# Left and right token half by turns for each weight tile, in place of one half after the other

## The reference

```python
def layer(x, ...):
    h = rmsnorm(x, norm_mix_g)
    p = h @ w_in                                # 2048 x 5120
    u = gelu(p[u]); v = rmsnorm(gelu(p[v]), sgu_norm_g)
    y_a = u * chunk_sgu(v, w_s, b_s)
    zc, new_mix = causal_dwconv(cg * xb, mix_prev, conv_mix_w, conv_mix_b)
    y = concat(group_rmsnorm(y_a), group_rmsnorm(bg * zc))
    x = x + y @ w_out                           # 2048 x 2048
    h = rmsnorm(x, norm_ffn_g)
    gate, new_ffn = causal_dwconv(h @ w_gate, ffn_prev, conv_ffn_w, conv_ffn_b)   # 2048 x 5632
    x = x + (silu(gate) * (h @ w_up)) @ w_down  # 2048 x 5632, 5632 x 2048
    return x, new_mix, new_ffn, v
```

## Time and profile before

| | us |
|---|---|
| median of 3 runs | 2511.51 |
| lowest, highest | 2509.65, 2513.96 |
| span of the profiled execution | 2507.9 |
| TensorE busy | 2462.1 (98%) |
| VectorE busy | 1206.8 (48%) |
| ScalarE busy | 617.1 (25%) |
| GpSimd busy | 160.2 (6%) |
| mean DMA rate | 87 GB/s |

### The profile page before, as it was taken

How to read it: one execution, slowest core, us unless ns; L and a number is a source line. 1 busy time by engine, 2 the same in 40 slices (tenths; PEclk the granted TensorE clock), 3 DMA queues, 4 the chain that set the end, 5 groups by cost and what they waited for, 6 DMA issues and landing times.

```text
span 2507.9 us, 45612 instructions
## 1 busy us (share of the span) xinstructions
PE 2462.1 (98%) x18473; PEld 2452.1 (98%) x18473; DVE 1206.8 (48%) x1902; ACT 617.1 (25%) x738; POOL 160.2 (6%) x279
## 2 busy tenths in 40 slices
PE   6999999999999999999999999999999999999996
PEld 6999999999999999999999999999999999999996
DVE  6357644556224535455434444444544354454445
ACT  6224312113113322222212222122222211222224
POOL 3310000001221000000000000000000000000004
PEclk8999999999999999999999999999999999999998
DMA  5422222224222222223222222222232222222222
GB/s 153 159 84 71 69 85 85 83 85 151 83 79 73 84 80 81 84 84 92 75 84 84 84 84 81 80 80 82 78 97 78 76 84 84 84 84 84 84 85 84
DMA packets 326837, 219.17 MB, mean 87 GB/s; under 512 B 6804, under 2 KB 301839, under 8 KB 324992
## 3 DMA queue, kind: packets, MB, share of 16 engines
q1 hardware_dynamic: 324432, 203.98, 27.2%
q0 software_dynamic: 2352, 14.41, 1.6%
HBM read 208.19 MB, written 10.18 MB: 87 GB/s over the span
## 4 chain that ended last, share of the span: by engine, by line
PE 96%; ACT 1%; DVE 1%; POOL 0%; issue 0%; DMA 0%; POOLq 0%; SPq 0%; DVEq 0%; ACTq 0%
PE ps L1161 32%; PE ps L1163 31%; PE ps L1162 31%; DVE h_lo L797 0%; POOL acc L470 0%; ACT ps L540 0%; PE ps L1284 0%; ACT h_hi L512 0%; PE ps L1297 0%; DMA x_nat<-in_x_prompt_dram 0%; ACT X L520 0%; PE ps L1296 0%; ACT w_hi L491 0%; DVE rms L813 0%; PE ps L1276 0%
## 5 line engine op out<-in xcount | busy, mean ns | idle before, releaser
L1161 PE MATMUL ps<-h_hi,w_hi 128*128 128x288 f32 x4608 | 1362.2, 296 | 6.2 <-issue 4.9
L1163 PE MATMUL ps<-h_hi,w_lo 128*128 128x288 f32 x4608 | 1358.7, 295 | 0.0
L1162 PE MATMUL ps<-h_lo,w_hi 128*128 128x288 f32 x4608 | 1358.3, 295 | 0.0
L1161 PEld LDWEIGHTS ps<-h_hi,w_hi 128*128 128x128 f32 x4608 | 865.6, 188 | 8.4 <-issue 5.8
L1162 PEld LDWEIGHTS ps<-h_lo,w_hi 128*128 128x128 f32 x4608 | 865.7, 188 | 0.0
L1163 PEld LDWEIGHTS ps<-h_hi,w_lo 128*128 128x128 f32 x4608 | 865.7, 188 | 0.0
L771 DVE TENSOR_TENSOR w_lo<-raw,w_hi 128x1024 fp32r<-128x1024 f32 x376 | 460.5, 1248 | 305.7 <-ACT w_hi L491 305.6
L491 ACT ACTIVATE w_hi<-raw 128x1024 fp32r<-128x1024 f32 x376 | 384.2, 1050 | 489.9 <-PE ps L1163 474.5
L1161 PE MATMUL ps<-act_hi,w_hi 128*128 128x288 f32 x1408 | 418.4, 297 | 1.0 <-DVE scaled L781 1.0
L1163 PE MATMUL ps<-act_hi,w_lo 128*128 128x288 f32 x1408 | 415.0, 295 | 0.0
L1162 PE MATMUL ps<-act_lo,w_hi 128*128 128x288 f32 x1408 | 414.3, 294 | 0.0
(11 more groups left out here) (184 smaller groups left out, 921.6 us busy)
## 6 DMA issues: line engine op xcount, KB each, us to landing
raw<-in_w_gate_dram SPq DMA_DIRECT2D x88, 512.0 KB, 3.9
raw<-in_w_up_dram SPq DMA_DIRECT2D x88, 512.0 KB, 3.8
raw<-in_w_down_dram SPq DMA_DIRECT2D x88, 512.0 KB, 4.3
raw<-in_w_in_dram SPq DMA_DIRECT2D x80, 512.0 KB, 4.3
raw<-in_w_out_dram SPq DMA_DIRECT2D x32, 512.0 KB, 4.0
xT_scratch<-X POOLq DMA_DIRECT2D x1, 4608.0 KB, 18.5
X<-xT_scratch POOLq DMA_DIRECT2D x4, 1152.0 KB, 5.6
x_nat<-in_x_prompt_dram SPq DMA_DIRECT2D x4, 1024.0 KB, 8.6
```

Of the source, the lines that this page charges most:

```text
L1161: te.matmul(out, whi, xhi, start=start, stop=False)
L1162: te.matmul(out, whi, xlo, start=False, stop=False)
L1163: return te.matmul(out, wlo, xhi, start=False, stop=stop)
```

## The change

The helper `three` becomes `three_pairs`: it takes both halves of the input and makes the three products of the left half, then the three of the right half, for one weight tile. `gemm` and `down_tile` call it block by block, so the bank changes with every third matmul. In `gemm` the wait for the second piece moves from the 25th matmul to the 49th, and the signal for the first piece from the 72nd to the 48th. The hooks stay at the same counts. `gemm2_by_k` calls the new helper too, and its order is the same as before. The first gemm of the kernel, which starts before all of x is there, gets a function of its own with the old order. The order of the sums for each output value is as before.

```diff
-            def three(out, whi, wlo, xhi, xlo, start, stop):
-
-                te.matmul(out, whi, xhi, start=start, stop=False)
-                te.matmul(out, whi, xlo, start=False, stop=False)
-                return te.matmul(out, wlo, xhi, start=False, stop=stop)
-
-            def gemm(q, c, p, q1=None, mid=None, q3=None):
-
+            def three_pairs(p, whi, wlo, xhi, xlo, start, stop):
 
                 for half in range(2):
                     cols = slice(half * HALF, (half + 1) * HALF)
-                    for s in range(2):
-                        if half == 0:
-                            pe.wait_ge(lo_ready, q + s + 1)
-                        for k in range(PK):
-                            kk = s * PK + k
-                            last = three(pair(p, half), w_hi[:, (c + s) % 4, k, :], w_lo[:, (c + s) % 4, k, :],
-                                         h_hi[:, kk, cols], h_lo[:, kk, cols], kk == 0, kk == KT - 1)
-                        if half == 1:
+                    te.matmul(pair(p, half), whi, xhi[:, cols], start=start, stop=False)
+                    te.matmul(pair(p, half), whi, xlo[:, cols], start=False, stop=False)
+                    last = te.matmul(pair(p, half), wlo, xhi[:, cols], start=False, stop=stop)
+                return last
+
+            def gemm(q, c, p, q1=None, mid=None, q3=None):
+
+
+                for s in range(2):
+                    pe.wait_ge(lo_ready, q + s + 1)
+                    for k in range(PK):
+                        kk = s * PK + k
+                        last = three_pairs(p, w_hi[:, (c + s) % 4, k, :], w_lo[:, (c + s) % 4, k, :],
+                                           h_hi[:, kk, :], h_lo[:, kk, :], kk == 0, kk == KT - 1)
+                        hook = (q1, q3)[s] if k == PK // 2 - 1 else mid if s == 0 and k == PK - 1 else None
+                        if k == PK - 1:
                             last.then_inc(piece_done, 1)
-                        hook = (q1, mid, q3, None)[2 * half + s]
                         if hook is not None:
                             hook()
+
+            def first_gemm(q, c, p, mid):
+
+                for half in range(2):
+                    cols = slice(half * HALF, (half + 1) * HALF)
+                    for kk in range(KT):
...
@@
-                        for half in range(2):
-                            cols = slice(half * HALF, (half + 1) * HALF)
-                            last = three(pair(tile, half), w_hi[:, c, k, :], w_lo[:, c, k, :],
-                                         h_hi[:, kk, cols], h_lo[:, kk, cols], kk == 0, kk == KT - 1)
+                        last = three_pairs(tile, w_hi[:, c, k, :], w_lo[:, c, k, :],
+                                           h_hi[:, kk, :], h_lo[:, kk, :], kk == 0, kk == KT - 1)
@@
-            gemm(0, 0, 0, mid=rest_of_x)
+            first_gemm(0, 0, 0, rest_of_x)
@@
-                for half in range(2):
-                    cols = slice(half * HALF, (half + 1) * HALF)
-                    for k in ks:
-                        last = three(pair(p, half), w_hi[:, slot, 4 * k + jj, :], w_lo[:, slot, 4 * k + jj, :],
-                                     act_hi[:, k, cols], act_lo[:, k, cols], k == 0, k == 1)
+                for k in ks:
+                    last = three_pairs(p, w_hi[:, slot, 4 * k + jj, :], w_lo[:, slot, 4 * k + jj, :],
+                                       act_hi[:, k, :], act_lo[:, k, :], k == 0, k == 1)
```

More of the change, by code:

```diff
@@ L1178, in gemm @@
                             last.then_inc(piece_done, 1)
-                        hook = (q1, mid, q3, None)[2 * half + s]
                         if hook is not None:
                             hook()
+            def first_gemm(q, c, p, mid):
+                for half in range(2):
+                    cols = slice(half * HALF, (half + 1) * HALF)
+                    for kk in range(KT):
+                        s, k = kk // PK, kk % PK
+                        if half == 0 and k == 0:
+                            pe.wait_ge(lo_ready, q + s + 1)
+                        w, lo = w_hi[:, c + s, k, :], w_lo[:, c + s, k, :]
+                        te.matmul(pair(p, half), w, h_hi[:, kk, cols], start=kk == 0, stop=False)
+                        te.matmul(pair(p, half), w, h_lo[:, kk, cols], start=False, stop=False)
+                        last = te.matmul(pair(p, half), lo, h_hi[:, kk, cols], start=False, stop=kk == KT - 1)
+                        if half == 1 and k == PK - 1:
+                            last.then_inc(piece_done, 1)
+                    if half == 0:
+                        mid()
```

## The result

The changed kernel takes 2523.67 us (median of 4 runs, 2523.22 to 2524.16), beside 2511.1 us for the kernel before (4 runs, 2509.65 to 2513.96): 12.6 us more. The ratio is 1.0047, with a 95% interval of 1.0033 to 1.0061. The forecast was 2524.6 us.

A forecast was written before the change was run, and what follows sets the result against it. The prediction took TensorE's start-to-start matmul distance to bound the kernel. Its terms, 11.1 + 2.4 - 0.4 = +13.1 us on a 2507.9 us span, gave 2521.0, or 2524.6 us as median, range 2517 to 2527 us (0.79).

The forecast's parts named there:

- What bounds the kernel: Whole kernel: TensorE busy 98% of 2507.9 us, so the start-to-start distance over 18048 matmuls decides the time.
- gemm, +11.1 us: In gemm, 13344 matmuls go from 132.50 to 133.33 ns, the distance read in gemm2_by_k: +11.1 us.
- The price of down_tile: Rival for gemm and down_tile: each pair of bank changes costs 3.1 ns, +7.6 us in all, 2519.1 us; chance 0.19.
- down_tile, +2.4 us: In down_tile, 348 tiles of twelve matmuls go from 1593.1 to 1600.0 ns each: +2.4 us.
- The second piece's wait, -0.4 us: In the second gate tile, TensorE's wait at the 25th matmul for the second weight piece goes away: -0.4 us.
- Earlier release, both banks opened at once, hooks: 0: In gemm, first piece released 3.2 us earlier, right bank opened with the left, hooks at unchanged counts: each costs 0.
- The sum: Whole kernel: 11.1 + 2.4 - 0.4 = +13.1 us on the 2507.9 us span, so 2521.0; median 2524.6 us.
- More changes of bank, longer distance.: Across gemm, down_tile and gemm2_by_k, more frequent bank changes lengthen the distance: 132.50, 132.76 and 133.33 ns.
- The free change: Rival: bank change costs nothing, gemms stay at 132.50 ns, decided by under 132.9 ns; 2511.1 us; chance 0.13.
- the dearer visit: Rival: returning to a bank after three matmuls costs twice gemm2_by_k's price, +26.6 us, 2538 us; chance 0.05.
- The gain of both halves at 131.7: Rival in gemm: right half falls to the left half's distance, 6672 matmuls gain 1.4 ns, -9.3 us, 2501.8 us; chance 0.03.

The follow-up runs named there:

- the cut at 272: Kernel before in its own order, tokens cut at column 272 (left 272, right 304 columns) instead of evenly: 2495.65 us, ratio 0.9935.
- gemm alone: Against the changed kernel, down_tile put back in the old order, gemm kept in the new: 2521.62 us, ratio 1.0042 to the kernel before.
- twelve: Against the kernel before, gemm changes its half after every twelfth matmul, down_tile as before: 2510.15 us, one run.
- the columns alone: Against the changed kernel, streamed columns still change every third matmul but the bank stays, results not the reference's: 2524.2 us, one run.
- down_tile alone: Against the kernel before, down_tile put in the new order, gemm kept in the old: 2514.88 us, ratio 1.0012.
- six: Against the kernel before, gemm changes its half after every sixth matmul, down_tile as before: 2517.28 us, one run.
- the two terms: Two runs with the new order in one place only: in gemm, 2521.62 us, and in down_tile, 2514.88 us.

## Why the prediction was right

- **What bounds the kernel.** Right: only the distance between matmuls moved the time. No other engine's busy time changed.
- **gemm, +11.1 us.** Right in size: 133.33 ns, taken from gemm2_by_k, is what the gemms of the steady blocks now show. The price of down_tile (+6.9 us) was the wrong row to read from, since the cost of a change grows as the visit shortens. The 131.9 ns of the left half was read over one half of 48, where rows of 0.01 us are too coarse; over many it is 131.67.
- **down_tile, +2.4 us.** 1600 against 1593.3 ns (132.78 x 12), so 348 x 6.67 ns = +2.3 us. Right.
- **The second piece's wait, -0.4 us.** Right: TensorE was 6.03 us behind the kernel before at the 24th matmul of that gemm (828.03 and 822.00) and 5.63 us at the 26th (828.30 and 822.67).
- **Earlier release, both banks opened at once, hooks: 0.** Right, by the full blocks without idle time.
- **The sum.** The span was forecast at 2521.0 and came at 2522.5. Two pieces of it don't belong to the change. A DMA of parameters (bias_b) landed 8.2 us after its issue where it took 7.3 before, and TensorE, at the same place in both programs, stood behind it and went on 0.8 us later. Kernels with the order of before show that wait too: 1.1 us with the left columns for both halves, 1.6 with the cut at 272. And a stretch at the lower clock in this execution cost 1.2 us. Without the two the spans are 12.6 us apart, as the medians are, and the forecast of 13.1 is 0.5 us off; where that half microsecond lies was not found. The forecast of the median, 2524.6 us, came within 0.9 us of 2523.67, partly by luck: half of the 3.6 us that it added to the span was the lead of one short run, the one that the profile before happened to catch.
- **"More changes of bank, longer distance."** This is the step that is wrong; the number doesn't show it. gemm2_by_k told the size of the cost because it changes columns exactly as often as the new order does, not because it changes banks. I noted that the two halves differ in bank and in columns and that the time line can't say which matters, and then argued with the bank alone. The change's own description invites that. So the size was right by a sound choice of row, and the mechanism beside it was false: the bank is free (131.67 ns with a change every third matmul), and the start of the streamed columns costs (133.33 ns with the bank kept).
- **The rivals.** The free change is refuted as a forecast: it was to decide under 132.9 ns and 133.33 came. In its claim on the bank it was right. But it looked for the 133.33 ns of gemm2_by_k in the semaphore wait, the four banks or the place in the program, and an unbroken gemm with two banks shows the same distance; what was left out was the columns. Refuted too is the dearer visit, which had gemm2_by_k's price double. The gain of both halves at 131.7 did not come either, and for the reason given there against it. The section "Back-to-back issue gap" of the Trainium skill's page "TensorE: Matmul & The Clock Gate" has no term for the bank; on that the runs agree with it (131.67 ns with a change every third matmul and without), but the 122.5 ns that are an estimate by its formula for 288 columns are passed by 9.2 to 10.8 ns, and it has no term for where the streamed columns start either.

What stays open: why the fast half falls to the slow half's distance in visits of three and nearly keeps its own in visits of six and twelve, and what sets the steps of the distance (the overhead over width and start has a pattern that these runs tabulate and don't explain). That the start of the operand in SBUF matters is shown; a mechanism in SBUF or in TensorE is not. The table of starts is for rows of 2304 bytes; rows of another length were not run, and for visits of three only the starts 0 and 288 at 288 columns were read.

## What to carry to other kernels

When TensorE is busy throughout, measure the distance from start to start over a hundred matmuls for each stretch of the program that differs in shape, start or order; 1% hides there, and the mean duration of a matmul doesn't show it (296 ns before and 297 after for w_hi on h_hi). If a stretch has the order of the planned change already, its distance gives the size, but changing one thing at a time gives the cause: here bank and operand start changed together, and the bank was free. Try the cut of the columns as well as the order of the work: in this kernel a pair of 304 + 272 columns took 1.5% less than 288 + 288 (261.1 and 265.0 ns), and an even cut is only one choice. Measure each cut; neither the table of starts nor that of widths foretold this one.

## What I had not expected of the hardware

- The start of the streamed operand within a row changes the distance of a 288-column fp32r matmul between 131.67 and 133.33 ns, and the width changes what comes on top of the width at 2.4 GHz: 11.0 ns at 304 columns, 13.3 at 320, 14.0 at 512, all from column 0.
- Fast and slow starts (columns 0 and 288) mixed in visits of three make all matmuls slow: 133.33 ns.
- After TensorE had stood idle for 2.9 us ahead of the first gate and up tile, at the same place in both programs, the granted clock stayed up in the profile of before and fell in that of the changed kernel: to 0.60 of full speed over the stretch below, with matmuls 0.24 us apart where they are 0.13 at the upper level, so to the lower level (1.2 GHz) for most of it. Before, then after, in the columns of the earlier trace rows:

```profile
791.90:795.30 3.40, 3.33 (x23) 3.13 (x24) 3.40 (x4) 3.40 (x6) 1.44 (x2) 1.00 0.02 5
```

```profile
796.70:800.10 3.40, 3.38 (x16) 3.40 (x17) 3.40 (x4) 3.40 (x6) 1.41 (x2) 0.60 0.02 5
```

16 matmuls ran where 23 did, and the dip cost 1.2 us. It isn't tied to the new order. The runs with gemm alone and with twelve show it there (0.91 over the 19 us from 786), but so do runs in the order of before: with the banks exchanged, with the left columns for both halves, with the cut at 272 (0.91 each). The run with the columns alone, in the new order, has no dip there, nor has the run with down_tile alone. After an earlier wait, of 2.0 us ahead of w_out, some profiles have one as well, here that with six:

```profile
587.00:590.50 3.50, 3.50 (x19) 3.50 (x18) 3.40 (x7) 3.17 (x5) 0.00 (x0) 0.58 0.02 5
```

That it goes with the execution shows best in the fourteen runs of the kernel before that stand beside the runs of the two terms: one program, 2509.55 us where the mean granted clock was 0.992 and 2513.97 where it was 0.989. So single runs differ by a few microseconds that go with the clock, and a difference of one or two between single runs tells nothing of the order.
